# State-space core: the products that read the scanned state alternate between the two row halves and their two banks

## The chip, the cores and the metric

The kernel runs on one core of one Trainium2 chip. The metric is the device time of one execution in microseconds; less is better. The time before is the median of three runs.

## The reference, cut to what matters

The reference is a model of four layers on 512 tokens of width 1024: two attention layers, a state-space layer with a feed-forward layer, and a stick-breaking attention layer with a feed-forward layer. The change lies in the state-space core of the third layer:

```python
def s5_mixer(xn, w_in, ...):
    u = (xn @ w_in).astype(f32)
    ...
    def chunk_step(h0, u_t):
        bu = jnp.einsum('tbgh,gph->tbgp', u_t.astype(jnp.complex64), b_bar)
        a_cum, s = lax.associative_scan(binop, (a_elems, bu), axis=0)
        s = s + a_cum * h0[None]
        y = jnp.einsum('tbgp,ghp->tbgh', s, c_mat).real
        return s[-1], y
    ...
    g = jax.nn.gelu(y + d_skip * u)
    val, gate = jnp.split(g @ w_glu, 2, axis=-1)
    return val * jax.nn.sigmoid(gate)
```

There are 64 groups of 16 channels, each with 64 complex states.

## The kernel before, in words

The sequence of 512 tokens is cut into 64 blocks of 8 tokens (NSUP = 64). Within a block the output comes from a Toeplitz product with the inputs; between blocks it comes from the state at the block's end, which VectorE scans. The 1024 channels are 8 tiles, k = 0 to 7, of 8 groups each. One tile has 4 pairs of groups (g = 0 to 3), and of each pair one group's states lie in partitions 0 to 63 and the other's in partitions 64 to 127 (a = 0 and 1, the row halves). c = 0 and 1 are the real and the imaginary part.

For each tile k there are these steps:

- **V** (line 2339): TensorE makes the blocks' inputs to the state from U, into one PSUM bank. 32 products, each with 64 weight columns; the four of a pair go to the two column halves of the array.
- VectorE turns, scans and turns back (lines 1874 to 1885), and gives the state S.
- **Y, first part** (line 2319): 16 products over all 128 rows, 8 into the bank of a = 0 and then 8 into the bank of a = 1.
- **Y, second part** (line 2325): 32 products that read the scanned state. Each takes the 64 rows of one half a, 128 weight columns and 63 moving columns, and adds to the bank of its half. The last one of each half tells that its bank is ready.
- ScalarE evicts the two banks in turn (line 1373), SyncE stores the tile to DRAM (line 853), and for two tiles at a time eight DMAs bring it back, transposed (line 860). ScalarE applies the gelu and makes the high part (lines 1382, 1386), VectorE the low part (line 1889).

All small products here are in plain float32. The large ones (lines 2108 to 2110, three for each product) are in split precision with 512 moving columns.

The four banks X are handed out in one ring, in program order: the function `bank` waits until the user four places earlier has been evicted. Both banks of a tile are asked for before its first product.

The order on TensorE is written out by hand. The core has slots t = 0 to 19. Slots 0 to 7 lie between the blocks of the second input product (line 2108, kind s5u), 8 to 11 stand alone (the stage `between`), and 12 to 19 lie between the blocks of the first product with w_glu. Two tables say what a slot holds, the Y of a slot before its V:

```python
S5_V = {2: (0,), 3: (1,), 4: (2, 3), 7: (4, 5), 9: (6,), 10: (7,)}
S5_Y = {6: (0,), 7: (1,), 8: (2,), 9: (3,), 10: (4,), 11: (5, 6), 13: (7,)}
S5_GELU = {10: (0, 1), 11: (2, 3), 14: (4, 5), 15: (6, 7)}
```

In slot t ScalarE evicts the Y of slot t - 1. SyncE's queue holds, in this order: the stores of U for tiles 4 and 5, their loads, the store of Y for tile 0, the store of U for tile 6, the store of Y 1, the store of U 7, the loads of U 6 and 7, the loads of Y 0 and 1, the stores of Y 2 and 3, their loads, a weight load, the stores of Y 4 and 5, their loads, the stores of Y 6 and 7, their loads, a weight load. The Y of tile 7 is followed on TensorE by 45 large products (three blocks of 12, and 9 of the next), and then comes the first one that needs tile 7.

Of the kernel before, what the change touches and what calls it, by code (L numbers as in the profile page):

```python
# [136 lines left out]
def build(nc, w, out, upto=None):  # L137
# [3 lines left out]
    with ExitStack() as ctx:  # L141
# [439 lines left out]
        NSUP, NPAIR = SEQ // 8, 32  # L581
# [38 lines left out]
        def s5_S(k):  # L620
            return big[:, k, :]
# [7 lines left out]
        def s5_P(k):  # L629
            return attf[:, 1024 * k:1024 * k + 1024].rearrange("p (g c n) -> p g c n", g=4, c=2)  # L630

        def s5_ZL(k):
            o = 512 * (16, 20, 0, 4)[k % 4]
            return attf[:, o:o + 2048]
# [110 lines left out]
        def at_(*key):  # L745

            return sems[key[0]], counts.of[key]

        def by(*key):

            given = counts.given.get(key[0], 0) + 1
            assert counts.of[key] == given, (key, counts.of[key], given)
            counts.given[key[0]] = given
            return sems[key[0]], 1
# [1343 lines left out]
        def _(pe):  # L2098
            def bank(a):

                if a >= 4:
                    pe.wait_ge(*at_(*freed[a - 4]))
                return X[:, a % 4, :]

            def three(out, lhs, rhs, start, stop):

                (lh, ll), (rh, rl) = lhs, rhs
                pe.matmul(out, lh, rh, start=start, stop=False)  # L2108
                pe.matmul(out, lh, rl, start=False, stop=False)  # L2109
                return pe.matmul(out, ll, rh, start=False, stop=stop)  # L2110
# [72 lines left out]
            def pe_slot(s, t):  # L2183
# [6 lines left out]
                if s.akind == "s5":  # L2190
                    return pe_s5(s, t)
# [114 lines left out]
            def pe_s5(s, t):  # L2306


                for k in S5_Y.get(t, ()):
                    pe.wait_ge(s5_zl_loaded[k % 4], 32 * (k // 4 + 1))  # L2310
                    pe.wait_ge(*at_("s5_s", s.i, k))
                    b = [bank(s.aux["y", k, a]) for a in range(2)]
                    Z = s5_ZL(k)[:, 0:1024].rearrange("p (c g n) -> p c g n", c=2, g=4)
                    L = s5_ZL(k)[:, 1024:2048].rearrange("p (g a n) -> p g a n", g=4, a=2)
                    U = big[:, 8 + k, :].rearrange("p (g a j) -> p g a j", g=4, a=2)
                    S = s5_S(k).rearrange("p (c g j) -> p c g j", c=2, g=4)
                    for a in range(2):
                        for g in range(4):
                            pe.matmul(b[a][:, NSUP * g:NSUP * g + NSUP], L[:, g, a, :], U[:, g, a, :],
                                      start=g == 0, stop=False)  # L2320
                    for a in range(2):
                        r = slice(64 * a, 64 * a + 64)
                        for g in range(4):
                            for c in range(2):
                                ins = pe.matmul(b[a][:, NSUP * g + 1:NSUP * g + NSUP], Z[r, c, g, :],
                                                S[r, c, g, 0:NSUP - 1], start=False, stop=g == 3 and c == 1)
                        ins.then_inc(*by("aux_ready", s.aux["y", k, a]))
                for k in S5_V.get(t, ()):
                    if k == 0:
                        pe.wait_ge(s5_p_loaded, 16 * KT)  # L2330
                    pe.wait_ge(s5_u_loaded[k // 2 * 2 if k > 1 else k], 16 * 8)
                    b = bank(s.aux["v", k])
                    U = big[:, 8 + k, :].rearrange("p (g j) -> p g j", g=8)
                    for g in range(4):
                        for a in range(2):
                            r = slice(64 * a, 64 * a + 64)
                            for c in range(2):
                                o = 256 * c + NSUP * g
                                ins = pe.matmul(b[r, o:o + NSUP], s5_P(k)[:, g, c, r], U[:, 2 * g + a, :],
                                                start=True, stop=True)  # L2340
                    ins.then_inc(*by("aux_ready", s.aux["v", k]))
# [3 lines left out]
            for c in range(3):  # L2345
                ins = pe.transpose(bank(s5lam.aux)[:, 32 * c:32 * c + 32], s5_rows[:, c, :], ident[0:NPAIR, 0:NPAIR])
# [4 lines left out]
            for s in plan:  # L2351
# [6 lines left out]
                elif s.kind == "chunk":  # L2358
                    for u in range(s.nu):
# [4 lines left out]
                        for j in range(4):  # L2364
# [11 lines left out]
                            for k in ks:  # L2376
# [6 lines left out]
                                if s.wtype == "T":  # L2383
                                    c = slice(m * P, (m + 1) * P)
                                    ins = three(G[:, m, :], (W[0][:, c], W[1][:, c]), (u_hi[:, K, :], u_lo[:, K, :]),
                                                K == 0, K == KT - 1)
                                else:
                                    tok = m % 2 if s.wtype == "mem" else m
                                    c = slice(tok * P, (tok + 1) * P)
                                    x_hi, x_lo = s.us or (u_hi, u_lo)  # L2390
                                    ins = three(G[:, m, :], (x_hi[:, K, c], x_lo[:, K, c]), W, K == 0, K == KT - 1)
# [6 lines left out]
                            if s.x is not None and u == 1 and j == 3:  # L2398
                                pe.wait_ge(par_loaded, 16 * (len(loads) - 2))
                                for k in range(3):  # L2400
                                    ins = pe.transpose(bank(gains)[:, k * P:(k + 1) * P], vec[:, k, :], ident[:, :])
# [5 lines left out]
                elif s.kind == "down":  # L2407
                    for p, (col, ks) in enumerate(s.seq):
                        n, l = s.n + p, s.load_at[p]
                        begin, end = p % len(s.groups) == 0, (p + 1) % len(s.groups) == 0  # L2410
                        for m in range(4):
# [4 lines left out]
                            for j, k in enumerate(ks):  # L2416
                                if m == 0:
                                    pe.wait_ge(*at_("u_ready", s.i, l, k))
                                    pe.wait_ge(w_lo_done, lo_before[n] + j + 1)
                                c = slice(m * P, (m + 1) * P)  # L2420
                                ins = three(G[:, m, :], (u_hi[:, 4 * (l % 2) + j, c], u_lo[:, 4 * (l % 2) + j, c]),
                                            (w_hi[:, n % HL, j, :], w_lo[:, n % HL, j, :]),
                                            begin and j == 0, end and j == len(ks) - 1)
# [3 lines left out]
                elif s.kind == "forget":  # L2427
                    b = bank(s.aux)[0:C_HEADS, :]
                    for k in range(KT):
# [3 lines left out]
                        ins = three(b, (wc_hi[:, k, :], wc_lo[:, k, :]), (u_hi[:, k, :], u_lo[:, k, :]), k == 0, k == KT - 1)  # L2433
# [4 lines left out]
                elif s.kind == "s5c":  # L2438
                    pe.wait_ge(s5_c_loaded, 64)
                    for k in range(4):  # L2440
                        b = bank(s.aux[k])
                        for q in range(4):
                            o = P * (4 * (k % 2) + q)
                            ins = pe.transpose(b[:, q * P:(q + 1) * P], s5_crow[k // 2][:, o:o + P], ident[:, :])
# [24 lines left out]
```

## Time and profile before

| | |
|---|---|
| median of three runs | 2479.04 us |
| lowest and highest run | 2476.58, 2479.55 us |
| profiled execution | its time is told only as its span, 2477.0 us |
| TensorE matmul busy | 2359.4 us, 95% |
| VectorE, ScalarE, GpSimd busy | 1391.1, 1007.9, 264.8 us |
| mean granted TensorE clock | 0.963 |

Busy time is the time in which at least one instruction of the kind runs. A granted clock of 1.00 is 2.4 GHz, 0.50 is 1.2 GHz. The mean time of one matmul in the tables is longer than the spacing of two, since they overlap in the pipeline; what a group of matmuls takes is read from its busy time or from its start and end.

### The profile page before, as it was taken

To read this page: it belongs to the slowest core of one execution; us is meant where nothing else is said; L and a number is where in the kernel's file an instruction comes from. 1 tells how busy PE (TensorE), PEld (TensorE's weight loads), DVE (VectorE), ACT (ScalarE), POOL (GpSimd) and SP (SyncE) were. 2 spreads that over 40 slices of the span, in tenths; PEclk is the share of its full clock that TensorE was granted. 3 is DMA by queue.
4 is the path that set the end of the run, shared out by engine and by line. 5 is a ranking of instruction groups with operands and counts; after the bars stand their busy time and mean duration, and the time that the engine had idled before them with its cause. 6 is when DMAs were issued, how large, how long until landed. Compare 5 with 4: busy or idle time off the path is not lost. (4 is left out here: it accounts for less than half of the span.)

```text
span 2477.0 us, 29950 instructions
## 1 busy us (share of the span) xinstructions
PE 2359.4 (95%) x11031; PEld 1884.0 (76%) x11031; DVE 1391.1 (56%) x2921; ACT 1007.9 (41%) x1888; POOL 264.8 (11%) x350
## 2 busy tenths in 40 slices
PE   4999999899999999989899999999999999999999
PEld 3777777588777787767788888888878547888887
DVE  6966675856745455443553455554554585555543
ACT  4644645433444545443323333233344563333232
POOL 3641000025100111100000000000011230000000
PEclk8999999899999999999967999999999899999999
DMA  6454112134332222215462232232322102232222
GB/s 177 131 166 134 55 51 85 35 103 142 114 99 69 81 90 69 90 51 181 134 195 86 86 101 87 92 96 85 119 82 89 35 1 69 85 92 95 86 86 102
DMA packets 192797, 236.68 MB, mean 96 GB/s; under 512 B 38827, under 2 KB 120194, under 8 KB 192654
## 3 DMA queue, kind: packets, MB, share of 16 engines
q1 hardware_dynamic: 170910, 211.93, 26.9%
q10 hardware_dynamic: 21744, 22.84, 3.0%
q8 instruction: 90, 1.47, 0.2%
q14 instruction: 53, 0.43, 0.1%
HBM read 215.84 MB, written 23.09 MB: 96 GB/s over the span
## 5 line engine op out<-in xcount | busy, mean ns | idle before, releaser
L2108 PE MATMUL G<-w_hi,u_hi 128*128 128x512 f32 x1536 | 626.8, 408 | 12.1 <-issue 5.6
L2110 PE MATMUL G<-w_hi,u_lo 128*128 128x512 f32 x1536 | 604.5, 394 | 0.0
L2109 PE MATMUL G<-w_lo,u_hi 128*128 128x512 f32 x1536 | 603.3, 393 | 0.0
L1647 DVE SCALAR_TENSOR_TENSOR w_lo<-raw,par,w_hi 128x512 fp32r<-128x512 f32 x496 | 369.7, 785 | 414.7 <-ACT w_hi L1120 411.8
L2108 PE MATMUL G<-u_hi,w_hi 128*128 128x512 f32 (+1 forms) x1168 | 462.9, 396 | 11.8 <-DVE u_lo L1713 11.8
L1120 ACT ACTIVATE w_hi<-raw,par 128x512 fp32r<-128x512 f32 x496 | 317.5, 715 | 379.2 <-PE G L2110 370.5
L2109 PE MATMUL G<-u_lo,w_hi 128*128 128x512 f32 (+1 forms) x1168 | 451.1, 386 | 0.0
L2110 PE MATMUL G<-u_hi,w_lo 128*128 128x512 f32 (+1 forms) x1168 | 450.6, 386 | 0.0
L2108 PEld LDWEIGHTS G<-w_hi,u_hi 128*128 128x128 f32 x1536 | 291.7, 190 | 80.7 <-issue 13.4
L2110 PEld LDWEIGHTS G<-w_hi,u_lo 128*128 128x128 f32 x1536 | 291.2, 190 | 63.7
L2109 PEld LDWEIGHTS G<-w_lo,u_hi 128*128 128x128 f32 x1536 | 292.0, 190 | 61.2 <-issue 2.5
L2108 PEld LDWEIGHTS G<-u_hi,w_hi 128*128 128x128 f32 x1168 | 224.4, 192 | 66.2 <-DVE u_lo L1713 12.5
L2110 PEld LDWEIGHTS G<-u_hi,w_lo 128*128 128x128 f32 x1168 | 224.4, 192 | 43.9
L2109 PEld LDWEIGHTS G<-u_lo,w_hi 128*128 128x128 f32 x1168 | 224.4, 192 | 42.6 <-issue 1.4
L1116 ACT ACTIVATE w_hi<-raw 128x2048 fp32r<-128x2048 f32 (+1 forms) x52 | 96.1, 1849 | 295.8 <-PE G L2110 283.0
L1091 POOL TENSOR_TENSOR work<-att 128x512 f32<-128x512 f32 x62 | 67.2, 1085 | 1194.0 <-ACT att L1130 1193.9
L1642 DVE TENSOR_TENSOR w_lo<-raw,w_hi 128x512 fp32r<-128x512 f32 x200 | 137.9, 737 | 94.3 <-ACT w_hi L1116 94.2
L1720 DVE TENSOR_TENSOR u_lo<-big,u_hi 128x512 fp32r<-128x512 f32 x132 | 83.4, 694 | 142.6 <-ACT u_hi L1167 142.6
L1231 ACT ACTIVATE att<-att,small 128x256 f32<-128x256 f32 (+3 forms) x112 | 62.4, 558 | 81.3 <-DVE small L1801 80.8
L1211 ACT ACTIVATE att<-X 128x256 f32<-128x256 f32 (+3 forms) x112 | 46.7, 417 | 106.9 <-PE X L2228 106.3
L2228 PE MATMUL X<-ident,att 128*128 128x128 f32 x264 | 50.0, 284 | 33.7 <-DVE att L1813 16.6
L1182 ACT ACTIVATE att<-X,par 128x512 f32<-128x512 f32 x56 | 38.6, 689 | 97.2 <-PE X L2117 93.0
(297 smaller groups left out, 2513.4 us busy)
## 6 DMA issues: line engine op xcount, KB each, us to landing
raw<-in_ffn_w_up SPq DMA_DIRECT2D x88, 512.0 KB, 4.7
raw<-in_e_w_in SPq DMA_DIRECT2D x56, 512.0 KB, 4.7
raw<-in_o_w_in SPq DMA_DIRECT2D x56, 512.0 KB, 4.6
raw<-in_ffn_w_down SPq DMA_DIRECT2D x40, 512.0 KB, 4.5
raw<-in_e_w_out SPq DMA_DIRECT2D x16, 512.0 KB, 4.6
raw<-in_o_w_out SPq DMA_DIRECT2D x16, 512.0 KB, 4.4
raw<-in_a_w_glu SPq DMA_DIRECT2D x16, 512.0 KB, 4.3
raw<-in_w_kv SPq DMA_DIRECT2D x16, 512.0 KB, 4.4
```

Of the source, the lines that this page charges most:

```text
L1091: pool.tensor_tensor(sq[:, m, :], x, x, ALU.mult).then_inc(*by(s.squares, s.i, m))
L1116: nc.scalar.activation(w_hi[:, n % HL, 0:kn], raw[:, n % RAW, 0:kn], ACT.Copy).then_inc(w_hi_done, 1)
L1120: nc.scalar.activation(w_hi[:, n % HL, k], raw[:, n % RAW, k], ACT.Copy, scale=gain(name, k0 + k))\
L1211: nc.scalar.activation(att[:, 20:20 + nb, i * P:(i + 1) * P], X[:, a % 4, 0:nb * P].rearrange("p (a b) -> p a b", b=P), ACT.Copy).then_inc ...
L1231: ins = nc.scalar.activation(S, src, ACT.Exp, bias=nmx[:, c:c + 1], accum_out=rs[:, c:c + 1])
L1642: V.tensor_tensor(w_lo[:, n % HL, k], raw[:, n % RAW, k], w_hi[:, n % HL, k].bitcast(F32), ALU.subtract).then_inc(w_lo_done, 1)
L1647: V.scalar_tensor_tensor(w_lo[:, n % HL, k], raw[:, n % RAW, k], gain(name, k0 + k), w_hi[:, n % HL, k].bitcast(F32), ALU.mult, ALU.subtract)\
L1720: V.tensor_tensor(u_lo[:, 4 * (l % 2) + j, :], big[:, k, :], u_hi[:, 4 * (l % 2) + j, :].bitcast(F32), ALU.subtract).then_inc(*by("u_ready ...
L2108: pe.matmul(out, lh, rh, start=start, stop=False)
L2109: pe.matmul(out, lh, rl, start=False, stop=False)
L2110: return pe.matmul(out, ll, rh, start=False, stop=stop)
L2228: ins = pe.transpose(b[:, j * P:(j + 1) * P], S[:, j * P:(j + 1) * P], ident[:, :])
```

## The change

The 32 products of line 2325 are issued in another order. Before, all 16 of the first row half came and then all 16 of the second. Now each product of the first half is followed by the one of the second half with the same g and c. The operands, the banks and the number of products stay; each bank still adds up in the same order. The signals stay on the last product of each half, which are now the last two of the burst.

```diff
-                    for a in range(2):
-                        r = slice(64 * a, 64 * a + 64)
-                        for g in range(4):
-                            for c in range(2):
+                    for g in range(4):
+                        for c in range(2):
+                            for a in range(2):
+                                r, last = slice(64 * a, 64 * a + 64), g == 3 and c == 1
                                 ins = pe.matmul(b[a][:, NSUP * g + 1:NSUP * g + NSUP], Z[r, c, g, :],
-                                                S[r, c, g, 0:NSUP - 1], start=False, stop=g == 3 and c == 1)
-                        ins.then_inc(*by("aux_ready", s.aux["y", k, a]))
+                                                S[r, c, g, 0:NSUP - 1], start=False, stop=last)
+                                if last:
+                                    ins.then_inc(*by("aux_ready", s.aux["y", k, a]))
```

## Rows read from the trace of the kernel before

**Rows 1.** The page, part 1: busy time, share of the span, instructions.
```profile
PE 2359.4 (95%) x11031; PEld 1884.0 (76%) x11031; DVE 1391.1 (56%) x2921; ACT 1007.9 (41%) x1888; POOL 264.8 (11%) x350
```

**Rows 2.** Groups by line, PE: line, operation, shapes, count | busy us, mean ns | idle before.
```profile
L2325 PE MATMUL X<-big,att 64*128 64x63 f32 x256 | 45.4, 390 | 0.0
...
L2319 PE MATMUL X<-big,att 128*128 128x64 f32 x128 | 23.9, 366 | 3.5 <-ACT work L1373 3.5
...
L2339 PE MATMUL X<-big,att 128*64 128x64 f32 x256 | 13.0, 282 | 4.9 <-issue 4.8 <-DMA big<-s_u 0.2
```

**Rows 3.** Windows of the core: length, busy (x count) of each engine, granted clock.
```profile
1260.05:1263.40 3.35, 3.30 (x61) 3.30 (x63) 1.20 (x2) 0.00 (x0) 0.00 (x0) 0.50 0.43 165
1263.50:1266.60 3.10, 3.10 (x19) 2.25 (x15) 2.93 (x6) 0.00 (x0) 0.00 (x0) 1.00 0.00 0
1270.10:1323.10 53.00, 52.93 (x304) 51.56 (x304) 20.87 (x36) 11.38 (x18) 0.00 (x0) 0.50 0.53 144
...
1328.35:1335.10 6.75, 6.75 (x50) 6.56 (x48) 0.00 (x0) 0.38 (x1) 0.00 (x0) 0.75 0.01 2
```

**Rows 4.** Timeline of PE: start, length, line, what, count, idle before it.
```profile
1270.17 3.55 PE L2319 MATMUL X<-big,att 128*128 128x64 f32 x16 [3.50 <-ACT work L1373]
1273.66 6.29 PE L2325 MATMUL X<-big,att 64*128 64x63 f32 x32
...
1289.71 2.03 PE L2339 MATMUL X<-big,att 128*64 128x64 f32 x32
...
1316.88 6.29 PE L2325 MATMUL X<-big,att 64*128 64x63 f32 x32
```

**Rows 5.** Line 2325 on PE in 1276.75:1277.15 and in 1278.25:1278.65.
```profile
L2325 PE MATMUL X<-big,att x6: 417/417/417, 1276.5 to 1277.0; 64*128 64x63 f32 x6
...
L2325 PE MATMUL X<-big,att x3: 417/417/417, 1278.0 to 1278.5; 64*128 64x63 f32 x3
```

**Rows 6.** Timeline of ACT: evictions of the banks of tile 2 and tile 7.
```profile
1277.37 0.38 ACT L1373 ACTIVATE work<-X 128x256 f32<-128x256 f32 x1 [7.34 <-PE X L2325]
1279.99 0.38 ACT L1373 ACTIVATE work<-X 128x256 f32<-128x256 f32 x1 [2.24 <-PE X L2325]
...
1335.18 0.38 ACT L1373 ACTIVATE work<-X 128x256 f32<-128x256 f32 x1 [2.28 <-PE X L2325]
```

**Rows 7.** Windows, line 2325 alone, tiles 0, 1 and 7: length, busy, clock.
```profile
1243.00:1249.00 6.00, 4.09 (x32) 3.90 (x32) 0.78 1.02 385
1254.00:1260.05 6.05, 4.91 (x32) 4.72 (x32) 0.72 0.97 266
...
1330.00:1336.00 6.00, 4.96 (x32) 4.78 (x32) 0.64 0.01 3
```

**Rows 8.** Timeline of SP and PE around the V of tiles 4 and 5.
```profile
1249.44 4.83 SPq L848 DMA_DIRECT2D big<-s_u  x8
...
1260.10 3.62 PE L2339 MATMUL X<-big,att 128*64 128x64 f32 x64 [0.17 <-DMA big<-s_u]
```

**Rows 9.** Timeline of DVE: tile 7 and what follows it.
```profile
1303.56 0.69 DVE L1874 TENSOR_TENSOR work<-X,big 128x512 f32<-128x512 f32 x1 [4.25 <-PE X L2339]
...
1310.96 2.49 DVE L1642 TENSOR_TENSOR w_lo<-raw,w_hi 128x512 fp32r<-128x512 f32 x4
```

**Rows 10.** Timeline of SP, ACT and PE at the core's end.
```profile
1335.59 0.34 SPq L853 DMA_DIRECT2D s_y<-work  x1
1337.66 3.75 SPq L860 DMA_DIRECT2D big<-s_y  x8
...
1343.80 1.12 ACT L1382 ACTIVATE big<-big 128x512 f32<-128x512 f32 x1 [4.91 <-DMA big<-s_y]
...
1348.06 0.50 PE L2108 MATMUL G<-w_hi,u_hi 128*128 128x512 f32 x1 [0.73 <-DVE u_lo L1889]
```

**Rows 11.** Timeline of PE, the change from 128 rows to 64, clock 1.00.
```profile
1243.68 0.28 PE L2319 MATMUL X<-big,att 128*128 128x64 f32 x1
1243.89 0.32 PE L2325 MATMUL X<-big,att 64*128 64x63 f32 x1
```

## The prediction

> **What bounds the kernel now.** I read the page's shares first. TensorE is busy for 95% of the span and VectorE for 56% [rows 1], so the first question is whether TensorE is also what sets the end in the stretch of the change. The groups by line then give the size of what is edited: the 256 products of line 2325 cover 45.4 us, 8 bursts of 32 [rows 2]. The windows of the core show where they lie. From 1270.10 to 1323.10 TensorE is busy for 52.93 of 53.00 us, VectorE for 20.87 and ScalarE for 11.38, at a granted clock of 0.50 [rows 3]. That stretch holds five of the eight bursts, tiles 2 to 6, and the timeline shows them as equal pieces of 6.29 us, the first at 1273.66 and the last at 1316.88, with no idle time before them [rows 4]. There TensorE is the bound and every us that it saves counts, until another engine is late.
>
> The other three bursts are to be read one by one. Those of tiles 0 and 1 take 4.09 and 4.91 us [rows 7], but the V of tiles 4 and 5 behind them ends its wait at 1260.10 with a DMA, 0.17 us after TensorE had come free [rows 8]. Tile 7's takes 4.96 us [rows 7], and from its end a chain runs through the other engines: eviction, store, eight loads, gelu, and at 1348.06 TensorE, which had waited 0.73 us for it [rows 6, 10].
>
> **What one burst costs, and what in another order.** At half clock a burst runs 6.29 us. ScalarE's two evictions tell when each half was done: the first starts at 1277.37, the second at 1279.99 [rows 6]. So the first half ended 3.71 us after the burst's start at 1273.66, and the second only 2.62 us later, though it holds as many products. The second half must have started about 1 us before the first ended. The counts show it. In 0.40 us at the seam, six products of the line are under way, in 0.40 us later on, three [rows 5]: two row halves run at once, each at its own pace, and neither is slowed. A matmul that is not held by its own half passes the ones that are.
>
> With the halves alternating, both have work from the first product to the last. A burst then costs what one half costs alone, 3.71 us, and saves 2.62 us. A second estimate comes from V, whose products alternate between the column halves and have half as many weight columns: 64 take 3.62 us at the same clock [rows 8], 57 ns each. Twice that for twice the columns gives 113 ns, and 32 of these 3.62 us. I take the saving of 2.62 us. Its lower bound is a loss: with no overlap at all, the burst takes twice 3.71, or 7.4 us, 1.1 more than now. Its upper bound is that V's 57 ns hold here too, which gives 1.8 us for a burst and saves 4.5. I take the middle because it is this line's own pace, twice.
>
> The Trainium skill is split here. "TensorE: Matmul & The Clock Gate", Part 3 (What overlaps and what doesn't), says that matmuls start and end strictly in program order; "TensorEngine Tiling (Array Packing)", Key Properties, that different tiles can load and multiply in parallel. By the first, read strictly, the second half could not start before the first was through, and the burst of before would have taken 7.4 us; the trace has 6.29, so it agrees with the second.
>
> **The sum.** Five bursts at half clock: 5 x 2.62 = 13.1 us. Tile 7's burst: its second half was evicted 2.28 us after the first eviction of 0.38 us had ended [rows 6], so it saves 2.66. Together 15.8. Against that stands the second eviction. Now both banks are ready at once, ScalarE takes them one after the other, and the later one ends one eviction, 0.38 us, later after the burst's end than before. For tiles 2 to 6 this is covered: what TensorE does next is at least a V of 2.03 us or a first part of 3.6 us [rows 4], and the bank ring needs the bank only then. For tile 7 it lies on the chain to 1348.06. So 15.8 - 0.4 = 15.4.
>
> The bursts of tiles 0 and 1 save some 2.2 us each (4.09 to 1.9 at full clock, 4.91 to about 2.5), and I cost that at almost nothing: TensorE only comes earlier to the same DMA. Its loads are eight, issued from 1249.44 on for 4.83 us [rows 8], and SyncE's queue has waited for nothing of TensorE's that moves. Only the loads of weights for tile 4, which ScalarE issues behind the block after tile 0, come some 3 us earlier and so leave the rings freer at the end of these eight. That may let V start up to 2.5 us sooner, or not at all; I take 1.
>
> Is another engine late next? TensorE would reach the block with w_glu at 1323.1 - 13.1 = 1310.0. VectorE's work that it needs ends at 1310.96 + 2.49 = 1313.45 now. It hangs on V of tile 7, where VectorE waited 4.25 us for TensorE [rows 9]. That V comes three bursts earlier (tiles 2, 3, 4), 7.9 us, so this work ends at 1305.6, 4.4 us before it is needed. The loads of Y 2 and 3 hang on the store of tile 3 (two bursts, 5.2 us sooner), their gelu ends well before VectorE comes to it. At the end of the core the chain from tile 7's burst to 1348.06 stays 13 us long, and TensorE fills all of them but 0.73 us with 45 large products, as before.
>
> From 1348 on TensorE is full again, and all that follows moves as one. The profiled execution has a span of 2477.0 us, 2.0 below the median of the three runs. 2477.0 - 16.4 = 2460.6 as a span, and 2479.04 - 16.4 = 2462.6 as a time.
>
> **Rivals.** *The clock rises in the core.* The stretch of 53 us runs at 0.50 although TensorE is never idle, so these sparse products do not count as activity enough. V's do: after 3.3 us of nothing but V at 0.50 the clock rose at once, and the next block, 1263.5 on, had 1.00 [rows 3, 8]. An alternated burst is twice as dense as now, so it may raise the clock next to a V. For it speaks V; against it, that half of all the rest (line 2319, 3.6 us per tile) is as sparse as before. One rise of some 7 us at 1.00 gives 3.4 us back: 2459. If it rises often, VectorE's work, 4.4 us behind, is the next bound, and some 2 us more come after it: 2479.0 - 16.4 - 6.4 = 2456. The skill's page on TensorE (the table "Why this matters for your kernels") would have a TensorE without gaps at full clock; the 0.50 of this stretch contradicts that.
>
> *The gain is partly given back.* The halves overlap in part only, or the loads of Y lag, and half the gain stays: about 2470.
>
> *The change does nothing measurable.* The saved time is all waited for elsewhere, as it is for tiles 0 and 1: 2479. Against it stand the 52.93 us busy of 53.00 [rows 3], with no idle time before the bursts [rows 4].
>
> *Slower: each switch between the halves drains the array.* The switch from 128 rows to 64 has such a price: 0.21 us from the last start to the first [rows 11], where two products of a first part are 0.11 apart at that clock (3.55 us for 16 at half clock [rows 4]), so 0.1 a switch. With 31 switches a burst and no overlap, a burst would take 7.4 + 3.1 = 10.5 us, 4.2 more than now, and six of them 25 us: 2504. It decides as soon as the overlap is lost; with the overlap kept, a switch would have to cost 2.62 / 31 = 85 ns. Against it, V switches column halves after every second product at 57 ns each, and the seam shows no gap.
>
> **How the numbers follow.** My forecast (gain 12 to 18 us) has 0.62, the clock 0.20, partly given back (5 to 12 us) 0.08, nothing measurable 0.05, slower 0.05. The first is the likeliest: 2462.6. [...] The range takes in the clock case down to 2456, and at the upper end gains of 11 us, 2468; 0.82 of the chance lies inside. A measurement of this kernel can tell 0.2%, 5 us, from no change: faster 0.90, same 0.05, slower 0.05.
>
> **What would show it.** In the profile after, line 2325 covers 32 us or less instead of 45.4: bursts of 3.7 us at half clock, 1.9 at full. Six products are under way in 0.40 us in the middle of a burst. The two evictions of a tile follow each other without a wait. The V of tiles 4 and 5 has an idle time of 3 to 5 us before it, ended by a DMA. V of tile 7 leaves VectorE still waiting. The stretch from tile 2's first part to the first block with w_glu is 40 us. Before the product that needs tile 7 TensorE waits about a microsecond. It is wrong if bursts stay above 5 us, if TensorE is idle within the 40 us, or if the clock in it is not 0.50.

## The result

The changed kernel takes 2465.27 us in the median of four runs (2461.12 to 2467.89), the kernel before 2479.3 (2476.58 to 2481.35, four runs). The ratio is 0.9944, 95% interval 0.9932 to 0.9957: 14.0 us or 0.56% faster. 2462.6 was forecast, with a gain of 16.4. The profiled execution, timed at 2464.76 us, has a span of 2463.0, 14.0 below that of before.

In the page and the groups by line of the changed kernel, the line of the change and its neighbours (line, shapes, count | busy us, mean ns):

```profile
PE 2334.1 (95%) x11031; PEld 1859.5 (75%) x11031; DVE 1387.0 (56%) x2921; ACT 1009.7 (41%) x1888; POOL 263.0 (11%) x350
...
L2325 PE MATMUL X<-big,att 64*128 64x63 f32 x256 | 24.4, 366 | 0.0
L2319 PE MATMUL X<-big,att 128*128 128x64 f32 x128 | 23.6, 362 | 3.5 <-ACT work L1373 3.5
```

Line 2325 covers 24.4 us instead of 45.4 [rows 2], so 21.0 us of TensorE's time are gone, and two thirds of them show in the time. TensorE's timeline of the changed kernel tells where. Its columns are those of [rows 4]; line 2340 is the V of before, one line further down.

```profile
1241.32 1.89 PE L2319 MATMUL X<-big,att 128*128 128x64 f32 x16
1243.14 2.00 PE L2325 MATMUL X<-big,att 64*128 64x63 f32 x32
1247.94 1.89 PE L2319 MATMUL X<-big,att 128*128 128x64 f32 x16
1249.76 2.00 PE L2325 MATMUL X<-big,att 64*128 64x63 f32 x32
1259.21 3.73 PE L2340 MATMUL X<-big,att 128*64 128x64 f32 x64 [7.45 <-DMA big<-s_u]
1269.52 3.22 PE L2319 MATMUL X<-big,att 128*128 128x64 f32 x16 [3.49 <-ACT work L1373]
1272.67 3.68 PE L2325 MATMUL X<-big,att 64*128 64x63 f32 x32
...
1284.32 2.03 PE L2340 MATMUL X<-big,att 128*64 128x64 f32 x32 [0.76 <-DMA big<-s_u]
...
1306.27 3.68 PE L2325 MATMUL X<-big,att 64*128 64x63 f32 x32
...
1314.81 1.89 PE L2319 MATMUL X<-big,att 128*128 128x64 f32 x16
1316.63 2.00 PE L2325 MATMUL X<-big,att 64*128 64x63 f32 x32
```

The bursts of tiles 2 to 6 are 3.68 us, where [rows 4] has 6.29. Those of tiles 0 and 1 are 2.00 instead of 4.09 and 4.91 [rows 7], and behind them stands a wait of 7.45 us for the same loads as before. In the middle of a burst eight records of the line are under way in 0.40 us:

```profile
L2325 PE MATMUL X<-big,att x8: 417/418/418, 1274.0 to 1274.6; 64*128 64x63 f32 x8
```

That is the line's row in the window 1274.3:1274.7, against three or six in [rows 5].

A word on counting. The text ahead speaks of 32 products a burst; these are records. In the source there are 16, and each float32 product is two array instructions. The same holds for the 16 of the first part and the 32 of V. So the alternation is by pairs of records, with 15 changes of the half in a burst and not 31. V changes its column half after every second source product, four records.

To compare kernels, whose cores start at slightly different times, I count from the first part of tile 0. The starts are read from TensorE's timelines, in us after that point; "w_glu" is the first large product behind tile 6, "needs tile 7" is the twentieth product of line 2108 from there.

| | V 4, 5 | Y 2 | V 6 | w_glu | needs tile 7 | end |
|---|---|---|---|---|---|---|
| before | 18.0 | 28.1 | 47.6 | 81.0 | 106.0 | 1235.0 |
| changed | 17.9 | 28.2 | 43.0 | 68.6 | 91.6 | 1221.7 |
| changed, run again | 17.4 | 27.8 | 43.1 | 68.6 | 90.7 | 1224.0 |

To the start of tile 2 nothing is gained, 0.1 us is lost. From there to the block with w_glu it is 12.6 us, at tile 7 another 1.9, and 1.1 are given back behind it: 13.3 us. The rest of the 14.0 is the 0.75 us by which the core started earlier in this execution, ahead of the first product that the change touches.

Behind tile 7 two executions of one program differ by more than that. From the product that needs tile 7 to the end it is 1129.0 us before, 1130.0 in the first profile of the changed kernel and 1133.3 in the second.

### The profile page after: what moved, and what is told of

Its sections match the earlier page's. It is cut to its first block and busy times, and to the rows that moved or that the text cites. A ratio compares the mean times of both kernels' runs of the same rounds, so it can differ in the third digit from the quotient of the medians.

```text
span 2463.0 us, 29950 instructions
## 1 busy us (share of the span) xinstructions
PE 2334.1 (95%) x11031; PEld 1859.5 (75%) x11031; DVE 1387.0 (56%) x2921; ACT 1009.7 (41%) x1888; POOL 263.0 (11%) x350
```

## The experiments

Each changes a few lines of the changed kernel. "Before" is the kernel of before, run beside them on the same chip: 2477.67 us for runs 1 to 4, 2474.77 for runs 5 to 8, 2475.91 for runs 9 to 12. The first three experiments were timed once each, so there the verdict rests on the profile and not on the time.

### How the halves overlap

```diff
-                    for g in range(4):
-                        for c in range(2):
-                            for a in range(2):
+                    for g, c, a in [(p // 2, p % 2, a) for q in range(0, 8, N) for a in range(2) for p in range(q, q + N)]:
```

With N = 2 and N = 4; N = 1 would be the changed kernel, N = 8 that of before.

> The halves alternate in runs of two source products instead of one. Each float32 product is two array instructions in the trace (16 products, 32 records in a burst), so a run is four records. Theory A, two row halves run at once and a half's next records may start up to four records ahead of the other half's last ones, as the seam of the kernel before showed: the burst stays at 3.7 us at half clock and 2.0 at full. Rival B, a half must have its next record directly behind the other's: the burst grows to some 5 us at half clock.

> The halves alternate in runs of four source products (eight records). Theory A (a look-ahead of four records): three seams, of which each hides four of 32 records, so 20 spacings of 0.213 us and the first one, 4.5 us a burst at half clock, between 3.7 and 6.3. Rival B (no look-ahead but at the very end of a half): 6.3 us or more. Rival C (look-ahead of a whole run of eight): 3.7 us.

Measured: one burst of tile 2 in the timeline of the first and of the second.

```profile
1273.30 3.73 PE L2323 MATMUL X<-big,att 64*128 64x63 f32 x32
```

```profile
1274.25 4.71 PE L2323 MATMUL X<-big,att 64*128 64x63 f32 x32
```

At full clock they are 2.05 and 2.60 us. All four lengths of a run fit one reading. Take 0.213 us for a record of one half at half clock and some 0.27 us a burst beside; both are estimates, from 3.68 us for two chains of 16 records and from the 2.1 us between the first and the last of 11 records inside a half. Then 3.68, 3.73, 4.71 and 6.29 us are 16.0, 16.2, 20.8 and 28.3 spacings. With 32 records and a seam between runs that hides about four, runs of eight give 20 and runs of sixteen 28. Theory A holds: 3.73 us where 3.7 were expected (rival B had 5), and 4.71 where 4.5 were (rivals B and C had 6.3 and 3.7). A half gets ahead of the other's last records by some four records, no more, and the order in the program decides how much runs at once. The seven changes of half of the first of these kernels and the fifteen of the changed one cost alike (3.73 and 3.68 us), so a change of half has no price of its own that shows. The look-ahead is small, but it makes alternation in pairs of products as good as in single ones.

```diff
-                    for a in range(2):
-                        for g in range(4):
+                    for g in range(4):
+                        for a in range(2):
                             pe.matmul(b[a][:, NSUP * g:NSUP * g + NSUP], L[:, g, a, :], U[:, g, a, :],
```

> As the changed kernel, and the first part, whose products use all 128 rows, alternates between the two banks as well. Theory A, the gain of the change comes from the row halves of the array: the first part stays at 3.6 to 3.7 us at half clock and 1.9 at full, the total of its line at 23.6 us. Rival B, it comes from the alternation of the banks written: the first part falls too, to about 2 us at half clock, and its line to some 13 us.

The change alternates row halves and banks, so either could be the cause. Here the first part, on all rows, alternates banks too. From the groups by line of this kernel:

```profile
L2319 PE MATMUL X<-big,att 128*128 128x64 f32 x128 | 23.6, 362 | 3.5 <-ACT work L1373 3.5
```

The same 23.6 us as in the changed kernel. Alternating banks alone gives nothing to products that use all rows; the gain needs the two row halves. The reverse, two row halves into one bank, was not tried, so it is not shown whether the gain needs the two banks as well.

### Which tiles carry the gain

```diff
+                    for g, c, a in ([(p // 2, p % 2, a) for p in range(8) for a in range(2)] if k < 2 else [(p // 2, p % 2, a) for a in range(2) for p in range(8)]):
```

and the same with `1 < k < 7` and with `k > 1`.

> The halves alternate for tiles 0 and 1 only, all others in the order of before. Theory A, what these two save is lost at the wait of the V of tiles 4 and 5 for its loads: the time stays within 1.5 us of the kernel before, and the idle time before that V is 5 to 7 us. Rival B, the loads end sooner because the weight loads behind tile 0 are issued sooner: 2 to 3 us faster.

> The halves alternate for tiles 2 to 6 only. Theory A, these five carry the gain, 5 times 2.6 us less the 0.8 us by which the V of tile 6 waits for its loads: 12 us faster than before, 2 to 3 us slower than the full change. Rival B, the chain of stores and loads sets the core's end whatever TensorE does, and tile 7 carries the gain: under 5 us.

> The halves alternate for tiles 2 to 7; tiles 0 and 1 keep the order of before. Theory A, what tiles 0 and 1 save is not only lost at the wait for the loads, they also pull the weight loads of tile 4 into them: as fast as the full change or up to 3 us faster, with no idle time of TensorE before the V of tiles 4 and 5, or under 1 us. Rival B, the wait only takes in what was saved: equal to the full change within 1 us in every window behind that V.

Measured: tiles 0 and 1 alone, 2474.44 us, ratio 0.9989 (0.998 to 0.9998). That is 3.2 us less in the median, more than theory A's 1.5 and near rival B's 2 to 3; the interval, 0.5 to 5 us, does not tell them apart. The profiled execution took 2477.1 us, one of the longer of its eleven, and has no gain in it: V 4, 5 starts 17.7 us after the first part of tile 0 (18.0 before) and the span ends 1235.0 after it, as before. Rival B's reason does not show there: the V comes only 0.3 us sooner. The idle time is a little over theory A's 5 to 7 us:

```profile
1258.12 3.74 PE L2338 MATMUL X<-big,att 128*64 128x64 f32 x64 [7.26 <-DMA big<-s_u]
```

It is more than the 5.0 us that the two bursts save (9.0 to 4.0). The other 2.4 are those of the block of large products between them. Before, this row of the windows has it at half clock; in this kernel, as in the changed one, it takes 2.9 us at 1.00 and not 5.3:

```profile
1248.00:1253.20 5.20, 5.20 (x13) 4.04 (x14) 4.92 (x9) 0.00 (x0) 0.00 (x0) 0.50 0.59 198
```

So TensorE comes 7.4 us sooner to the same loads.

Tiles 2 to 6 alone: 2463.79 us, 0.9955 (0.9941 to 0.9969), 11.0 us faster where 12 were expected. Rival B of the second expectation is out. Tiles 2 to 7: 2463.70 us, 0.9946 (0.9934 to 0.9958); the full change again, beside it: 2465.16, 0.995 (0.9938 to 0.9962). Leaving tiles 0 and 1 as they were costs nothing measurable. The idle time before V 4, 5 is gone there, as theory A had it, and w_glu comes after 68.5 us as against 68.6, as rival B had it. The times do not decide between the two.

Between these two runs of tiles from 2 on, the steps up to tile 2 differ although the code there is the same: V 4, 5 at 16.3 and 17.9 us, Y 2 at 24.9 and 28.1. In the first, tile 1's burst fell on a granted clock of 1.00 (3.39 us), its V ran in 2.13 us, and nothing waited. So the same code can be 3 us apart at this place from one execution to the next, and differences of that size are read from several runs.

### Why the loads of U 4 and 5 did not come sooner

```diff
                     if k < 4:
-                        s5_load_zl(k + 4)
+                    for n in ((), (0, 1), (2,), (3,))[k] if k < 4 else ():
+                        s5_load_zl(n + 4)
```

> The full change, and ScalarE issues the weight loads for tile 4 behind those evictions of tile 1 instead of tile 0, together with tile 5's. Theory A, in the full change these 1 MB come 5 us sooner than in the kernel before and share the rings with the eight loads of U 4 and 5, which land 6 us after their issue instead of 2.5: without them the V of tiles 4 and 5 starts some 3 us sooner after the first part of tile 0 (14 to 15 us instead of 17.9), and the whole is 2 to 4 us faster than the full change. Rival B, the loads of U are slow for another reason (their own small packets, the table load): the V starts as late as in the full change.

The rows below are the line of these loads around their issue (issue times, then the landing, us from issue, min/median/max) of the kernel before, then of the changed one, then of this experiment.

```profile
L848 SPq DMA_DIRECT2D big<-s_u x8: 318/450/1512, 1249.4 to 1253.8; - x8
...
DMA to landing us min/median/max: 2.6/3.0/7.0
```

```profile
L848 SPq DMA_DIRECT2D big<-s_u x8: 319/448/1066, 1248.5 to 1252.4; - x8
...
DMA to landing us min/median/max: 4.8/6.8/7.7
```

```profile
L848 SPq DMA_DIRECT2D big<-s_u x8: 319/448/1223, 1250.4 to 1254.6; - x8
...
DMA to landing us min/median/max: 2.8/3.0/3.5
```

Theory A holds at the place. In the changed kernel ScalarE issues tile 4's two weight loads and a table at the same moment as SyncE its eight small ones:

```profile
1248.14 0.33 ACTq L1366 DMA_DIRECT2D big<-s_turn  x1
1248.56 0.39 ACTq L1347 DMA_DIRECT2D att<-s_out  x1
1248.98 1.38 ACTq L1348 DMA_DIRECT2D att<-s_toeplitz  x1
```

The eight then land in 6.8 us (median) instead of 3.0. With the weight loads put off they are back at 3.0, and V 4, 5 starts after 14.7 us instead of 17.9, Y 2 after 24.8 instead of 28.2. Rival B's table is not the cause, for ScalarE still issues it just ahead of the eight loads:

```profile
1249.80 0.33 ACTq L1366 DMA_DIRECT2D big<-s_turn  x1
```

The other profiles say the same. In the ten in which tile 0 alternates (in single products, or in runs of two or four) and tile 4's weight loads follow it, these eight loads land in 5.9 to 6.8 us (median); in the three that leave tile 0 in the old order, and in this experiment, in 2.8 to 3.0.

The whole is 2462.46 us, 0.994 (0.9927 to 0.9953), against 0.995 (0.9938 to 0.9962) for the full change beside it: 2.7 us less in the median, but the intervals overlap. The profile shows most of the 3.3 us leaving again, at two waits:

```profile
1283.85 2.03 PE L2340 MATMUL X<-big,att 128*64 128x64 f32 x32 [1.78 <-DMA big<-s_u]
...
1296.30 3.65 PE L2319 MATMUL X<-big,att 128*128 128x64 f32 x16 [1.25 <-ACT work L1373]
```

At w_glu 0.8 us of them are left (67.7 against 68.6). So theory A's mechanism is shown and its price is not: ending the contention gains little in this execution, since the next transfers set the next waits.

### The idle time before V 4, 5, and the core's end

```diff
-        S5_V = {2: (0,), 3: (1,), 4: (2, 3), 7: (4, 5), 9: (6,), 10: (7,)}
-        S5_Y = {6: (0,), 7: (1,), 8: (2,), 9: (3,), 10: (4,), 11: (5, 6), 13: (7,)}
+        S5_V = {2: (0,), 3: (1,), 4: (2, 3), 8: (4, 5), 9: (6,), 10: (7,)}
+        S5_Y = {6: (0,), 7: (1, 2), 9: (3,), 10: (4,), 11: (5, 6), 13: (7,)}
```

> The full change, and the Y of tile 2 moves from slot 8 to slot 7, before the block, and the V of tiles 4 and 5 from slot 7 to slot 8, behind it. TensorE has 7.45 us without work before that V in the changed kernel. Theory A, the Y of tile 2 (6.5 us there) fills them, the block then needs no loads, and all behind it comes 6 to 7 us sooner: 2458. Rival B, the V now waits for ScalarE's evictions behind the block and a weight split, and VectorE's scans of tiles 4 to 7 come later by as much: no gain, 2463 to 2466.

Measured: 2460.16 us, 0.9941 (0.993 to 0.9953). In its profile Y 2 runs at once and at full clock (2.00 and 2.00 us instead of 3.22 and 3.68), but V 6 now waits:

```profile
1257.98 2.71 PE L2340 MATMUL X<-big,att 128*64 128x64 f32 x64 [3.19 <-ACT work L1373]
...
1276.24 2.03 PE L2340 MATMUL X<-big,att 128*64 128x64 f32 x32 [8.34 <-DMA big<-s_u]
```

w_glu comes after 64.3 us, 4.3 sooner than in the changed kernel. The time does not show a gain over the full change: the interval overlaps those of its two runs (ratios 0.9944 and 0.995). It is neither theory in full. The V of tiles 4 and 5 does wait for ScalarE, 3.19 us, as rival B had it, but VectorE's scans are not what is late next, it is the loads of U 6 and 7. SyncE has them behind the store of Y 1, whose eviction ScalarE makes only after the block and a weight split.

```diff
-        S5_Y = {... 11: (5, 6), 13: (7,)}
+        S5_Y = {... 11: (5, 6), 12: (7,)}
```

> The full change, and the Y of tile 7 moves from slot 13 to slot 12, before the first block with w_glu. Theory A, the core's end hangs on the chain from tile 7's burst through store, loads and gelu, 14 us, and a block more of large products lies under it: the wait of 2.9 us before the products that need tiles 6 and 7 goes, but the burst and its first part run at half clock (7.3 instead of 3.8 us): 1 to 2 us faster than the full change. Rival B, the half clock costs as much as the wait did: no change.

Measured: 2464.53 us, 0.9956 (0.9944 to 0.9968), no gain against the full change's 0.9944 and 0.995. Rival B: the wait is gone, but Y 7 runs at half clock. The product that needs tile 7 comes after 90.5 us, as against 91.6 and 90.7.

> Both moves together, tile 2 and tile 7. Theory A: their gains add, 7 to 9 us under the full change, 2457. Rival B: only one of them shows.

Measured: 2459.04 us, 0.9933 (0.9921 to 0.9945), 1.1 us under the first move alone, with intervals that overlap. Theory A's sum is not there. That only one of the moves shows is rival B, as far as these runs can tell.

```diff
                     y_store(0)
                     u_store(6)
-                    y_store(1)
                     u_store(7)
                     u_load(6, 2)
+                    y_store(1)
                     y_load(0)
```

This goes on top of the move of tile 2, with tile 7 in its old slot.

> The full change with the Y of tile 2 before the block and the V of tiles 4 and 5 behind it, and in SyncE's queue the store of Y 1 moves behind the loads of U 6 and 7. With the order of slots alone, the V of tile 6 waited 8.3 us for these loads, which stood behind the store of Y 1 and with it behind ScalarE's eviction of it. Theory A, the loads now hang on the store of U 7 alone, the wait goes, and the stretch from tile 0's first part to the block with w_glu shrinks by another 6 to 8 us: 2452. Rival B, VectorE's scans, which start later, take the place of the wait: half of it or less is gained.

Measured: **2453.08 us, 0.9906 (0.9892 to 0.992)**, 22.8 us faster than before and 12.1 faster than the full change beside it. From its timeline:

```profile
1249.00 2.00 PE L2319 MATMUL X<-big,att 128*128 128x64 f32 x16
1250.93 2.00 PE L2325 MATMUL X<-big,att 64*128 64x63 f32 x32
1259.07 2.85 PE L2340 MATMUL X<-big,att 128*64 128x64 f32 x64 [3.19 <-ACT work L1373]
...
1270.47 2.03 PE L2340 MATMUL X<-big,att 128*64 128x64 f32 x32 [1.33 <-DMA big<-s_u]
...
1283.10 3.65 PE L2319 MATMUL X<-big,att 128*128 128x64 f32 x16 [1.43 <-ACT work L1373]
```

Of the 8.34 us before V 6, 1.33 stay, and 1.43 come up before Y 5. w_glu comes after 58.9 us, 5.4 sooner than without the SyncE move. Theory A in substance, 5.4 where it had 6 to 8; 1.4 us went into the new wait. This is the only variant whose interval lies apart from the full change's. The move in SyncE's queue was not tried without the slots, nor either of them without the change, so how much of the 12.1 us needs the faster products is not shown.

> The full change once more, on the chip and against the runs of before that the next three share. 12 to 15 us faster than before; every theory says the same of it.

Measured: 2465.16 us, 10.8 below before, less than the 12 to 15 expected. Its ratio of 0.995 (0.9938 to 0.9962, a gain of 9.4 to 15.4 us) overlaps the first one's (0.9932 to 0.9957, 10.7 to 16.9 us). The forecast's 16.4 lies inside the first interval and outside the second.

## Why the prediction was right, step by step

**Two row halves run at once.** Right. A saving of 2.62 us a burst at half clock was read from the seam of before, 2.61 were measured (6.29 to 3.68); twenty-eight spacings became sixteen. The length that the prediction wrote, 3.71 us, is the time to the first eviction. The seam bears more than was read from it: records that only start in program order would still have 32 spacings, some 7.1 us, so the 6.29 of before already needed starts out of order. The lower bound (no overlap) and V's pace as a gain of 4.5 us are both out. The second estimate, twice V's 57 ns, gave 3.62. That it came so near is no proof of its reason: whether V's column halves run at once, and whether the number of weight columns sets the pace, was not tested.

**Five bursts, 13.1 us.** Measured from Y 2 to w_glu: 12.6 (52.94 us before, 40.36 after). The step that was passed over is the V of tile 6. I asked whether VectorE or the loads of Y are late next, not whether the loads of U 6 and 7 are, and TensorE waited 0.76 us for them, as the timeline above shows. By the prediction's own words it is a sign of being wrong if TensorE is idle within the 40 us, and so it was, by little. In that stretch TensorE is busy for 39.62 of 40.45 us, at half clock as forecast:

```profile
1269.45:1309.90 40.45, 39.62 (x305) 38.18 (x305) 20.74 (x35) 10.66 (x17) 0.00 (x0) 0.51 0.73 186
```

**Tiles 0 and 1, 1 us.** Mis-sized: 0.1 at V 4, 5 and nothing at Y 2. That their saving is lost in the wait for the loads was right, but the wait is 7.45 us and not 3 to 5: the block between the two bursts, which ran at half clock before, was left out. Why I allowed 1 us for it was wrong in its sign: the weight loads that come sooner do not free the rings, they meet the eight loads of U. Putting them off made these land in 3.0 instead of 6.8 us.

**Tile 7, 2.66 less one eviction.** The burst gave 2.96 (4.96 to 2.00, at a kinder clock). ScalarE's evictions do follow each other now, as the step had it:

```profile
1318.66 0.66 ACT L1373 ACTIVATE work<-X 128x256 f32<-128x256 f32 x2 [8.02 <-PE X L2325]
```

From the burst's end to the product that needs tile 7 it was 12.9 us before and is 14.3 now (13.5 in the second profile of this kernel). With tile 7 in the old order and tiles 2 to 6 in the new one it is 13.1. The eviction explains 0.3 of this. The first of the eight loads of Y is issued 3.1 us after the burst's end (2.5 before), and the last has landed after 10.1 us (8.6 before). Why they land more slowly, by 0.9 us beside the later issue, stays open.

**All behind moves as one.** Not quite. TensorE was to wait about a microsecond before tile 7's product; it waited 2.93 us before tile 6's, and the granted clock then went to 0.50. The windows around it, and the timeline:

```profile
1326.00:1331.30 5.30, 2.38 (x11) 1.65 (x9) 0.69 (x1) 2.47 (x3) 0.00 (x0) 1.00 1.09 217
1331.45:1334.80 3.35, 3.27 (x7) 2.11 (x8) 1.38 (x2) 3.30 (x4) 0.00 (x0) 0.50 0.00 0
1334.85:1340.00 5.15, 5.15 (x24) 4.26 (x23) 3.43 (x7) 1.21 (x3) 0.00 (x0) 1.00 0.00 0
```

```profile
1331.32 0.71 PE L2108 MATMUL G<-w_hi,u_hi 128*128 128x512 f32 x1 [2.93 <-DVE u_lo L1889]
1331.83 0.63 PE L2109 MATMUL G<-w_lo,u_hi 128*128 128x512 f32 x1
```

Seven products fit where at full clock 14 would. From the product that needs tile 7, at 1332.97, to the end of that window it is 1.8 us at half the pace, which is some 0.9 of the 1.1 us given back behind it. A wait was in the sum, its price in clock was not. This holds for one execution. In the second profile a wait of 2.06 us is followed by half clock as well, and the stretch behind tile 7 is 3.2 us longer than here; with tile 7 moved ahead of the block there is neither wait nor half clock at this place, and that stretch, 1130.5 us, is no shorter.

**The signs.** Met were line 2325 (24.4 us, at most 32 forecast), the bursts of 3.7 us at half clock and about 1.9 at full (2.00), the evictions without a wait, VectorE still waiting for V of tile 7 (1.64 us), the 40 us and the half clock. Eight records and not six are under way in 0.40 us. Missed were the idle time before the V of tiles 4 and 5 (7.45 us, 3 to 5 forecast), the one within the 40 us (0.76, none forecast) and the one at the core's end (2.93 us, about 1 forecast).

**The rivals.** In the core's dense part the clock did not rise, 0.51 as against 0.50. At tiles 0 and 1 it was higher. In all nine profiles in which tile 0 alternates in single products, its burst and the block of large products behind it run at 1.00 (2.00 and 2.9 us); in the three of the old order the burst takes 4.05 to 4.36 us, the clock falls to half in it or behind it, and the block takes 5.0 to 5.3. The rival looked for a rise beside a V, and not here; what this gave went into the wait for the loads. At tile 7 an execution decides: with the old order its burst took 4.96 us in one profile and, at 1.00, 3.39 in another. Nothing speaks for a drain between halves.

"Partly given back" is what happened in small. Counted from tile 0 the profile gained 13.3 us of the 16.4. Missing are 1.1 at tiles 0 and 1, 0.5 in the five bursts (0.76 of waiting, less 0.3 by which tile 2's first part was faster), 0.4 at tile 7 and 1.1 behind it. The 0.75 us by which the core started earlier bring it to 14.0, and that is luck. Each of these terms comes from one execution, and executions differ by as much. The second run of the same kernel gained 10.8 us in the median, under the 12 to 18 of the forecast.

## What to carry to other kernels

Where products use half of the rows only, put the two halves next to each other in the program; in this kernel the other half's records started about four records ahead, no further. A seam between two halves in the present trace tells the new pace before anything is built: count the records under way there. And read each burst by the wait behind it: here three of eight stood before transfers. Once the products were fast, the order of the slots and of the queue that feeds them (12.1 us more for three edited lines) was worth as much as the change, 10.8 beside it.

## What was not expected of the hardware

- Records of a second row half start before records of the first that stand ahead of them in the program, about four of them, in the kernel of before already.
- At half clock and with 64 moving columns, V's records (64 weight columns) come at 57 ns each, 3.62 us for 64, and the alternated ones (128 weight columns) at 115 ns, 3.68 us for 32. What sets the pace is not shown.
- Eight loads of 64 KB in small packets, with 1.4 MB of another queue at the same moment, land in 6.8 us (median) instead of 3.0. With only the table's 0.4 MB of these beside them they land in 3.0.
- TensorE is busy for 39.62 of 40.45 us at a granted clock of 0.51, and for 52.93 of 53.00 at 0.50 before. The same bursts between blocks of large products run at 1.00, alternated.
